# The delta rule's triangular inverse in 64 by 64 diagonal blocks at levels two to six

## The reference, cut to what matters

```python
dec = jnp.exp(jnp.where(incl, diff, -jnp.inf))
kkt = jnp.einsum('bhtd,bhsd->bhts', kk, kk)
m = jnp.where(strict, bb[..., :, None] * kkt * dec, 0.0) + eye
rhs = jnp.concatenate([vv * bb[..., None], kk * (bb * jnp.exp(gam))[..., None]], axis=-1)
sol = lax.linalg.triangular_solve(m, rhs, left_side=True, lower=True, unit_diagonal=True)
u, w = sol[..., :dv], sol[..., dv:]
v_new = u - jnp.einsum('bhtd,bhde->bhte', w, S)
```

## Time and profile before

| what | us |
|---|---|
| median of 3 runs (1916.54 to 1918.02) | 1916.65 |
| the profiled execution | 1918.86 |
| its span | 1917.0 |
| TensorE matmul busy | 1758.6 |
| VectorE busy | 982.5 |
| ScalarE busy | 613.8 |
| GpSimd busy | 292.2 |

### The profile page before, as it was taken

How to read it: one execution, slowest core, us unless ns; L and a number is a source line. 1 busy time by engine, 2 the same in 40 slices (tenths; PEclk the granted TensorE clock), 3 DMA queues, 4 the chain that set the end, 5 groups by cost and what they waited for, 6 DMA issues and landing times.

```text
span 1917.0 us, 33325 instructions
## 1 busy us (share of the span) xinstructions
PE 1758.6 (92%) x13854; PEld 1660.4 (87%) x13854; DVE 982.5 (51%) x1544; ACT 613.8 (32%) x984; POOL 292.2 (15%) x339
## 2 busy tenths in 40 slices
PE   6889977799899999999999999688879999999996
PEld 5889845798699999999999997566679999999996
DVE  5489968643545444444553232477644544444443
ACT  4334545222432121222231235455523212121121
POOL 1136300132020000000010000677511000000001
PEclk8999979798999999999999999677779999999998
DMA  6112310100122222222222222111122222222221
GB/s 195 43 61 67 113 44 1 45 2 1 72 78 78 88 77 78 87 78 77 77 77 78 87 78 78 35 48 48 58 77 78 77 78 89 78 68 87 67 78 51
DMA packets 37203, 132.99 MB, mean 69 GB/s; under 512 B 4816, under 2 KB 7712, under 8 KB 36560
## 3 DMA queue, kind: packets, MB, share of 16 engines
q1 hardware_dynamic: 35552, 122.11, 19.4%
q0 software_dynamic: 1088, 6.25, 0.9%
q10 hardware_dynamic: 432, 2.73, 0.6%
HBM read 119.90 MB, written 10.84 MB: 68 GB/s over the span
## 4 chain that ended last, share of the span: by engine, by line
PE 77%; DVE 13%; ACT 4%; issue 3%; DMA 1%; POOL 1%; SPq 0%; DVEq 0%; ACTq 0%; POOLq 0%
PE ps L418 60%; PE ps L1681 3%; DVE arena L1245 1%; DVE arena L694 1%; DVE best L1247 1%; PE ps L885 1%; PE ps L906 1%; DMA h<-in_x 1%; PE ps L904 1%; DVE wsp L404 1%; PE ps L2074 1%; PE ps L2082 1%; PE ps L1199 1%; PE ps L960 1%; DVE arena L1948 1%
## 5 line engine op out<-in xcount | busy, mean ns | idle before, releaser
L418 PE MATMUL ps<-x_hi,wsp 128*128 128x296 f32 x4096 | 745.5, 303 | 36.3 <-DVE wsp L404 12.9
L418 PEld LDWEIGHTS ps<-x_hi,wsp 128*128 128x128 f32 x4096 | 621.7, 191 | 42.9 <-DVE wsp L404 20.7
L400 ACT ACTIVATE wsp<-ring 128x1024 fp32r<-128x1024 f32 x200 | 212.0, 1061 | 906.5 <-PE ps L418 882.5
L418 PE MATMUL ps<-x_lo,wsp 128*128 128x296 f32 x2048 | 449.1, 301 | 0.0
L418 PE MATMUL ps<-hid,wsp 128*128 128x296 f32 x3072 | 421.1, 299 | 0.0
L418 PEld LDWEIGHTS ps<-hid,wsp 128*128 128x128 f32 x3072 | 420.3, 189 | 0.0
L418 PEld LDWEIGHTS ps<-x_lo,wsp 128*128 128x128 f32 x2048 | 338.3, 192 | 0.0
L404 DVE TENSOR_TENSOR wsp<-ring,wsp 128x1024 fp32r<-128x1024 f32 x200 | 247.6, 1239 | 65.3 <-ACT wsp L400 64.6
L499 DVE TENSOR_TENSOR arena<-ps,arena 128x592 f32<-128x592 f32 x64 | 49.6, 775 | 221.7 <-PE ps L418 221.7
L561 DVE TENSOR_SCALAR sq<-ps 128x592 f32<-128x592 f32 x64 | 49.6, 774 | 216.5 <-PE ps L418 216.5
L299 POOL TENSOR_TENSOR rn<-sq 128x592 f32<-128x592 f32 x4 | 6.9, 1731 | 851.8 <-ACT sq L281 851.8
(11 more groups left out here) (346 smaller groups left out, 1974.6 us busy)
## 6 DMA issues: line engine op xcount, KB each, us to landing
ring<-in_w SPq DMA_DIRECT2D x200, 512.0 KB, 3.3
arena<-in_shgrn SPq DMA_DIRECT2D x8, 512.0 KB, 3.5
out_hgrn_s<-arena SPq DMA_DIRECT2D x8, 512.0 KB, 3.1
arena<-in_kvpages SPq DMA_DIRECT2D x16, 192.0 KB, 2.5
h<-in_x SPq DMA_DIRECT2D x4, 592.0 KB, 11.8
out_y<-xn SPq DMA_DIRECT2D x1, 2368.0 KB, 7.0
arena<-in_sdelta POOLq DMA_DIRECT2D x1, 2048.0 KB, 8.3
out_delta_s<-arena POOLq DMA_DIRECT2D x1, 2048.0 KB, 7.0
```

Of the source, the lines that this page charges most:

```text
L400: nc.scalar.activation(wsp[:, j % 2, 0, :], ring[:, j % SLOTS, :], ACT.Copy).then_inc(w_hi, 1)
L418: mm = nc.tensor.matmul(ps[:, 2 * (j % 2) + e, 0:HALF], a[:, k * P:(k + 1) * P], b[:, k, e * HALF:(e + 1) * HALF], start=(k == 0 and a is ...
```

## The change

A helper lists the parts of a step. Tile 0 and the last level keep one part, the whole tile; at level indices 1 to 5 tiles 1 to 4 get two, the rows 0 to 63 and 64 to 127. With such a slice `c` as the partitions and as the columns, each matmul, copy and subtraction is written once for each part, and what lies outside the two blocks is neither computed, copied nor subtracted. Semaphores are raised by the last part alone. GpSimd's mask product and level index 0 are untouched.

```diff
+        def parts_of(l, t):
+
+            if t == 0 or l == LEVELS - 1:
+                return [slice(0, ROWS[t])]
+            return [slice(0, P // 2), slice(P // 2, P)]
+
...
                         for hd in range(DNH):
-                            mm = nc.tensor.matmul(bank(n % 2, R, R)[:, hd], XL[n % 2][0:R, hd, 0:R],
-                                                  Ti[t][0:R, hd, 0:R], start=True, stop=True)
+                            for c in parts_of(l, t):
+                                mm = nc.tensor.matmul(bank(n % 2, R, R)[c, hd, c], XL[n % 2][c, hd, c], Ti[t][c, hd, c],
+                                                      start=True, stop=True)
...
                     if l < LAST[t]:
-                        nc.tensor.matmul(bank(2 + 2 * (m % 2), R, R)[:, hd], Tt[t][0:R, hd, 0:R],
-                                         P1[m % 2][0:R, hd, 0:R], start=True, stop=True)
-                    mm = nc.tensor.matmul(bank(3 + 2 * (m % 2), R, R)[:, hd], P1[m % 2][0:R, hd, 0:R],
-                                          Tt[t][0:R, hd, 0:R], start=True, stop=True)
+                        for c in parts_of(l, t):
+                            nc.tensor.matmul(bank(2 + 2 * (m % 2), R, R)[c, hd, c], Tt[t][c, hd, c], P1[m % 2][c, hd, c],
+                                             start=True, stop=True)
+                    for c in parts_of(l, t):
+                        mm = nc.tensor.matmul(bank(3 + 2 * (m % 2), R, R)[c, hd, c], P1[m % 2][c, hd, c],
+                                              Tt[t][c, hd, c], start=True, stop=True)
...
-                    nc.scalar.activation(P1[n % 2][0:R, :, 0:R], bank(n % 2, R, R), ACT.Copy)\
-                        .then_inc(sg("inv_p1"), 1)
+                    for c in parts_of(l, t):
+                        ins = nc.scalar.activation(P1[n % 2][c, :, c], bank(n % 2, R, R)[c, :, c], ACT.Copy)
+                    ins.then_inc(sg("inv_p1"), 1)
...
-                if l < LAST[t]:
-                    nc.vector.tensor_tensor(Ti[t][0:R, :, 0:R], Ti[t][0:R, :, 0:R], bank(2 + 2 * (n % 2), R, R),
-                                            ALU.subtract)
-                link(nc.vector.tensor_tensor(Tt[t][0:R, :, 0:R], Tt[t][0:R, :, 0:R],
-                                             bank(3 + 2 * (n % 2), R, R), ALU.subtract),
-                     "inv_used")
+                for c in parts_of(l, t):
+                    if l < LAST[t]:
+                        nc.vector.tensor_tensor(Ti[t][c, :, c], Ti[t][c, :, c], bank(2 + 2 * (n % 2), R, R)[c, :, c],
+                                                ALU.subtract)
+                    ins = nc.vector.tensor_tensor(Tt[t][c, :, c], Tt[t][c, :, c], bank(3 + 2 * (n % 2), R, R)[c, :, c],
+                                                  ALU.subtract)
+                link(ins, "inv_used")
```

## The result

The changed kernel takes 1882.1 us (median of 4 runs, 1881.08 to 1885.71) against 1917.3 for the kernel before beside it: a ratio of 0.982 [0.981, 0.984]. A second set of 5 runs gave 1880.5, 0.981 [0.980, 0.983]. The profiled execution took 1881.5 us (span 1879.7), 37.3 us less in the span than the one of before. In the kernel after, lines 868, 885, 904, 906, 918, 933, 935 and 960 have become 874, 892, 912, 915, 928, 944, 946 and 971.

What follows compares the result with a forecast made beforehand. TensorE bounds the inverse's stage at 2.68 us a step; with paired blocks at 1.39, VectorE sets 1.48. Summed over the levels, line 960 starts at 427.7 instead of 451.93: 1916.65 - 24.2 = 1892.5 us, range 1888 to 1904.

Steps and rivals of the forecast that it cites:

- What follows waits for this stage alone: Code behind the inverse's stage, from line 960 on: keeps its time, so the stage's 24.2 us come off the whole run.
- TensorE's part: Product steps at levels two to six, 128-row tiles: block pairs side by side at 0.058 us, 1.39 us instead of 2.68.
- The first rival: Blocks of a head wait for each other in one PSUM bank: step 2.78 us, nearly all near 1918.7; 6 in 100.
- VectorE as the next bound: Four 64x256 subtractions a step, starts 0.34 apart, last 0.41, some 0.05 handover: VectorE sets the step at 1.48 us.
- The last level: Inverse's last level: four unchanged steps of 1.79 us, 7.2 in all, then some 1.0 until line 960 at 427.7.
- the sum: Stage times added from 381.77 us: 389.9 with two level-two tiles done, level six ending 419.5, line 960 at 427.7.
- ScalarE and GpSimd as cover: Within a step: ScalarE's two copies, 0.77 us, hide under neighbouring steps' TensorE work; GpSimd's 1.09 lies below 1.48.
- no DMA is touched: Whole change: the waits keep their order, nothing new queues behind them, and DMA is left as it was.
- The second rival: TensorE's clock stays at 1.2 GHz through the stage with half the array used: 1923.7 us; 4 in 100.
- Its small part: Line 960's stretch: its 64 records at the lower clock throughout take 13.6 us instead of 10.9, +2.7.
- The third rival: Clock falls for a part, or pairs overlap by half: step near 2.0 us, 13.6 saved, 1903 us; 5 in 100.

Runs made afterwards that it cites:

- the changed stage with the standstills left in: The changed kernel with 64 more already-met wait instructions ahead of all others on TensorE: 1894.77 us, ratio 0.989.
- the second trace: The changed kernel run once more, unedited, in a later set and traced again: 1880.50 us.

## Why the prediction missed

**The step that failed** is "What follows waits for this stage alone": it let all behind the stage keep its time, and costed the 960 added TensorE instructions only where they run. They also move all code behind them by 3.75 pieces, and with that took the second MLP's loop out of the place where each turn fetched its code again. The missing term is 12.1 to 13.0 us in the traces, 12.7 to 14.3 between the medians above. It was to be seen in the trace of before: two pairs of idle gaps "<-issue" in a loop of otherwise unbroken work, beside 18 packets on an instruction queue. I read the chain and the stage, and never asked what TensorE waited for in the 60% of the chain on line 418. Nothing in the change aims at it: 64 idle instructions in the kernel before gain the same.

The Trainium skill, "Runtime: NRT & Kernel Launch", section "Instruction fetch mechanics", states blocks of 16 KiB, 256 instructions, and that a taken branch to a block outside the current window of two forces a fetch and stalls. The trace agrees on the pieces (18 packets, 0.29 MB) and that a loop's turn can stall; it differs on the window, for a loop of some 6.2 pieces turned without any fetch in the kernel after. The same section also gives TensorE 128 KiB, 2048 instructions, which is eight such pieces. With that the traces agree better: by the counts above a turn over seven pieces ran without a fetch, and one over eight did not.

**Without that term** the forecast holds: the changed stage with the standstills left in took 1894.8 us against 1892.5, and saved 22.4 us for 24.2. Point by point:
- TensorE's part: right. A pair takes 0.058 us, 0.107 at the lower clock, and 1.40 us a step where VectorE doesn't set it, for the forecast 1.39. The first rival, one after another in a shared bank, falls: two records in one bank start 3 to 36 ns apart, a pair every 0.058 us. The Trainium skill's rule in "TensorEngine Tiling (Array Packing)", section "Gotcha 1: PSUM Pressure", which would have left nothing, doesn't hold for these tiles, whose output partitions differ.
- VectorE as the next bound: right, its size off. 1.56 us a step for 1.48: between the second subtraction and the third, where the half of the partitions changes, starts lie 0.42 apart and not 0.34, and the handover to the next step takes 0.46. Levels five and six last 12.70 us (403.50 to 416.20) for 11.8.
- The last level: 9.6 us from 416.20 to line 971 for the 8.2 of the sum, which let the closing products of level six (16 pairs, 0.93 us) cost nothing beside it. Everything ahead of level five came out 0.4 shorter than summed. (The sum's 389.9 comes out with three, two and one of its terms, not with "three, one and two".) In all the stage saved 22.4 us, 23.5 in the second trace, for 24.2.
- ScalarE and GpSimd as cover: right. In the step shown the two copies end at 406.53 (405.76 and 0.77), and the product that reads them, line 912, starts at 407.22; GpSimd's 1.09 lies below 1.56. The words "no DMA is touched" were wrong for the instruction queue, as above.
- The second rival, the lower clock throughout: falls, the clock rose to 1.00 at 386.2, 10.5 us behind the stage's first product (7.5 in the second trace, whose stage is 1.1 shorter); the forecast had 10.9 (390.3, from 379.43). Its small part came true: line 971 ran more of its records at 0.50, +1.7 us in the first trace and +0.3 in the second, inside the +2.7 allowed. The third rival, part of the gain, falls too.

## What to carry to other kernels

A change that adds or removes instructions also moves the code behind it, and a hardware loop behind it can gain or lose by that: look for idle gaps "<-issue" at the loop's turns and for packets on the instruction queue within it, before and after. To part such a gain from the change's own, put as many instructions that do nothing ahead of the loop, in both kernels, and compare like with like. Half-size diagonal blocks paid here because they ran in pairs; the engine that drains them got twice the instructions and became the bound at once.

## What was not expected of the hardware

- TensorE stood still for 3.8 and 3.9 us at each turn of a loop that lay badly in its 16 KB pieces, and the clock fell to 0.50 behind it, so that the two turns cost 5.5 and 6.6 us; the same loop a quarter of a piece further on cost nothing.
- Two f32 64x64 products with different input and different output halves, written to one PSUM bank, overlapped fully: starts lie 3 to 36 ns apart in a pair, and a pair follows a pair every 0.058 us.
- VectorE starts two 64x256 subtractions from PSUM 0.34 us apart on the same half of the partitions and 0.42 apart, its whole length, where the half changes. Here the bank and the tile change back at the same place, so no run shows which of these it is.
